# Feed-forward pairs: four of seven products with 512 moving columns, and GpSimd adding sides and scaling gates

## The reference, cut to what matters

```python
def swiglu(x, w_in, w_out):
    gate, up = jnp.split(x @ w_in, 2, axis=-1)
    return (jax.nn.silu(gate) * up) @ w_out
...
h = swiglu(rmsnorm(x, norm_ffn1_pre[l]), w_ffn1_in[l], w_ffn1_out[l])
x = x + FFN_RESIDUAL_SCALE * rmsnorm(h, norm_ffn1_post[l])
```

## Time and profile before

| what | value |
|---|---|
| median of 3 runs | 1515.07 us (1514.86 to 1515.26) |
| the profiled execution's own time | 1514.94 us |
| its span, first to last instruction | 1513.3 us |
| TensorE busy | 1497.9 us, 99% |
| VectorE busy | 1071.1 us, 71% |
| ScalarE busy | 744.2 us, 49% |
| GpSimd busy | 54.2 us, 4% |
| DMA, mean | 101 GB/s |

### The profile page before, as it was taken

The page is one execution under the profiler, slowest core; times in us unless marked ns, Lnnn a source line. Parts: engine busy times, 40 slices in busy tenths (PEclk is TensorE's granted clock), DMA queues, the critical chain, the costliest instruction groups (busy, mean ns, idle before and its releaser), DMA issues.

```text
span 1513.3 us, 23600 instructions
## 1 busy us (share of the span) xinstructions
PE 1497.9 (99%) x9156; PEld 1343.9 (89%) x9156; DVE 1071.1 (71%) x1279; ACT 744.2 (49%) x1102; POOL 54.2 (4%) x101
## 2 busy tenths in 40 slices
PE   8999999999999999999999999999999999999998
PEld 7899998889988889899999888788888888889997
DVE  5888885326856847888886665788888865736873
ACT  6545443226566427544444234567676633344554
POOL 1000000001200002000000000100000000000001
PEclk9999999999999999999999999999999999999999
DMA  6233323232232222233335663222223132322331
GB/s 198 84 112 101 96 81 140 89 105 84 69 103 84 82 101 69 87 109 93 102 111 195 236 208 84 57 65 74 57 82 83 56 111 84 112 85 87 107 112 56
DMA packets 135044, 153.33 MB, mean 101 GB/s; under 512 B 3728, under 2 KB 123660, under 8 KB 134972
## 3 DMA queue, kind: packets, MB, share of 16 engines
q1 hardware_dynamic: 131712, 137.38, 28.9%
q0 software_dynamic: 3024, 14.88, 2.9%
q10 hardware_dynamic: 236, 0.06, 0.0%
HBM read 150.08 MB, written 2.23 MB: 101 GB/s over the span
## 4 chain that ended last, share of the span: by engine, by line
PE 96%; DVE 2%; ACT 1%; issue 0%; DMA 0%; DVEq 0%; ACTq 0%
PE ps L2532 20%; PE ps L2697 20%; PE ps L2534 19%; PE ps L2533 19%; PE ps L2702 10%; PE ps L2897 1%; PE ps L3003 1%; PE ps L3013 1%; PE ps L2983 1%; PE ps L2982 1%; PE ps L3012 1%; PE ps L2615 0%; PE ps L2964 0%; PE ps L2675 0%; DVE wl L1544 0%
## 5 line engine op out<-in xcount | busy, mean ns | idle before, releaser
L2532 PE MATMUL ps<-ah,wh 128*128 128x512 f32 (+1 forms) x1136 | 431.7, 380 | 3.8 <-DVE wl L1945 1.4
L2534 PE MATMUL ps<-ah,wl 128*128 128x512 f32 (+1 forms) x1136 | 425.6, 375 | 0.0
L2533 PE MATMUL ps<-al,wh 128*128 128x512 f32 (+1 forms) x1136 | 425.2, 374 | 0.0
L1544 DVE TENSOR_TENSOR wl<-raw,wh 128x2048 fp32r<-128x2048 f32 x59 | 135.2, 2291 | 191.2 <-ACT wh L831 191.0
L2532 PEld LDWEIGHTS ps<-ah,wh 128*128 128x128 f32 x1136 | 213.9, 188 | 43.3 <-issue 2.3
L2534 PEld LDWEIGHTS ps<-ah,wl 128*128 128x128 f32 x1136 | 213.8, 188 | 38.9
L2533 PEld LDWEIGHTS ps<-al,wh 128*128 128x128 f32 x1136 | 214.1, 188 | 35.5
L831 ACT ACTIVATE wh<-raw 128x2048 fp32r<-128x2048 f32 x60 | 114.7, 1911 | 236.7 <-PE ps L2534 233.0
L2697 PE MATMUL ps<-al,wh 128*128 128x256 f32 x704 | 172.7, 283 | 0.0
L2697 PE MATMUL ps<-ah,wh 128*128 128x256 f32 x704 | 172.7, 283 | 0.0
L2697 PEld LDWEIGHTS ps<-al,wh 128*128 128x128 f32 x704 | 135.2, 192 | 0.1
(11 more groups left out here) (436 smaller groups left out, 2535.6 us busy)
## 6 DMA issues: line engine op xcount, KB each, us to landing
raw<-in_w_ffn_in SPq DMA_DIRECT2D x74, 512.0 KB, 3.6
raw<-in_w_in SPq DMA_DIRECT2D x52, 512.0 KB, 4.4
raw<-in_w_ffn_out SPq DMA_DIRECT2D x22, 1024.0 KB, 5.0
ada_raw<-in_w_ada POOLq DMA_DIRECT2D x8, 1536.0 KB, 7.2
raw<-in_w_mix_in SPq DMA_DIRECT2D x10, 1024.0 KB, 5.4
raw<-in_w_ffn_in SPq DMA_DIRECT2D x7, 1024.0 KB, 5.3
raw<-in_w_in SPq DMA_DIRECT2D x6, 1024.0 KB, 5.6
raw<-in_w_mix_out SPq DMA_DIRECT2D x4, 1024.0 KB, 5.0
```

The costliest lines, as they stand in the source:

```text
L1544: nc.vector.tensor_tensor(wl[n % 2][:], raw[n % 2][:], wh[n % 2][:].bitcast(fp32), ALU.subtract).then_inc(lo_done, 2 if n + 1 in AHEAD else 1)
L2532: nc.tensor.matmul(bank, w[0], m[0], start=start, stop=False, skip_group_check=shared)
L2533: nc.tensor.matmul(bank, w[0], m[1], start=False, stop=False, skip_group_check=shared)
L2534: return nc.tensor.matmul(bank, w[1], m[0], start=False, stop=stop, skip_group_check=shared)
```

## The change

- `ah` and `al` become the two halves of one tile, `both`; `sh` and `sl` of `both_sums`.
- B11, T2, T3 and T4 of the two feed-forward blocks run through a new function, `sided`. Eight matmuls with `wh` move 512 columns each (256 of the high activations and 256 of the low), then eight with `wl` move 256. The result lies in two banks, one for each 128 weight columns (banks 0 and 1, or 6 and 7, by turns of the pair), each with a high side and a low side that must be added.
- ScalarE copies both sides of `up1` and `gate1`, the low side into `acc` and `h7` (`up1_side`, `gate1_side`), and after T4 the low side into `whole2` (`last_side`).
- GpSimd gets four operations a pair: `up1` plus its side, `gate1` plus its side, `gate2` times `rstd`, `gate1` times `rstd`.
- VectorE no longer scales gates. It adds both sides to `gate2`, the second add waiting for the first, and does so ahead of `gate1`, after the fifth product. The second half of `hidden` becomes an add and a multiplication.
- ScalarE takes silu of gate 2 first, and T4 and the next pair's T1 wait for other joins.

```diff
@@ GpSimd @@
+                def added(i, n, step, tile, side):
+                    pool.wait_ge(copied, i * 6 + (3 * n + step))
+                    nc.gpsimd.tensor_tensor(tile[:], tile[:], side, ALU.add).then_inc(side_added, 1)
+                def scaled(i, n, h, tile):
+                    pool.wait_ge(joined, i * 6 + (3 * n + 2 - h))
+                    nc.gpsimd.tensor_tensor(tile[:], tile[:], r_half[h], ALU.mult).then_inc(gate_ready, 1)
+                def pair(i, par):
+                    n = first + par
+                    added(i, n, 1, up1, up1_side)
+                    added(i, n, 3, gate1, gate1_side)
+                    scaled(i, n, 1, gate2)
+                    scaled(i, n, 0, gate1)
...
@@ ScalarE @@
+                def last_side(i, par):
+                    act.wait_ge(hid_ready, i * 2 + (f * NFO + PLAIN[f] + par))
+                    nc.scalar.activation(whole2[:], low_side(par % 2), ACT.Copy).then_inc(side_copied, 1)
...
+                    def sided_product(target, side):
+                        nc.scalar.activation(target[:], high_side(par % 2), ACT.Copy)
+                        nc.scalar.activation(side, low_side(par % 2), ACT.Copy).then_inc(copied, 1)
...
                         used(0)
+                        last_side(i, par - 1)
...
-                    product(up1, BANK1[par % 2])
+                    sided_product(up1, up1_side)
...
-                    product(gate1, BANK1[par % 2])
+                    sided_product(gate1, gate1_side)
                     high(6, i, n)
                     if end:
                         unit(0)
                         unit(1)
-                    gate(0)
                     used(5)
...
                         high(1, i, n + 1)
+                    gate(0)
@@ VectorE @@
+                        dve.wait_ge(side_copied, i * 2 + (n + 1))
+                        nc.vector.tensor_tensor(whole2[:], high_side(par % 2), whole2[:], ALU.add).then_inc(last_joined, 1)
+                        dve.wait_ge(last_joined, i * 2 + (n + 1))
+                        nc.vector.tensor_tensor(at, whole2[:], at, ALU.mult).then_inc(hid_ready, 1)
...
-                    def scaled(tile, h):
-                        dve.wait_ge(joined, i * 6 + (3 * n + h + 1))
-                        nc.vector.tensor_tensor(tile[:], tile[:], r_half[h], ALU.mult).then_inc(gate_ready, 1)
+                    def sided_join(tile):
+                        nc.vector.tensor_tensor(tile[:], high_side(par % 2), tile[:], ALU.add).then_inc(high_joined, 1)
+                        dve.wait_ge(high_joined, i * 2 + (n + 1))
+                        nc.vector.tensor_tensor(tile[:], low_side(par % 2), tile[:], ALU.add).then_inc(joined, 1)
...
-                    used(4)
+                    used(5)
+                    dve.wait_ge(copied, i * 6 + (3 * n + 2))
+                    sided_join(gate2)
                     dve.wait_ge(copied, i * 6 + (3 * n + 3))
+                    dve.wait_ge(side_added, i * 4 + (2 * n + 2))
                     join(gate1, BANK5)
@@ TensorE @@
+            def sided(f, i, n, k, par):
+                moving = both_of(f, PRODUCTS[k])
+                for nb in range(2):
+                    for kk in range(KD // 2):
+                        nc.tensor.matmul(ps[:, SIDE * par + nb, :].rearrange("p (s t) -> p s t", s=2), ring_of(wh, f, k)[:, kk, nb * P:(nb + 1) * P],
+                                         moving[:, :, kk, :], start=k == 0 and kk == 0, stop=False, skip_group_check=True)
+                pe.wait_ge(p_lo, i * 2 * PRODS + (PRODS * n + k + 1))
+                for nb in range(2):
+                    for kk in range(KD // 2):
+                        last = nc.tensor.matmul(ps[:, SIDE * par + nb, 0:T // 2], ring_of(wl, f, k)[:, kk, nb * P:(nb + 1) * P], moving[:, 0, kk, :],
+                                                start=False, stop=kk == KD // 2 - 1, skip_group_check=True)
```

More of the change, by code:

```diff
@@ L115 @@
 BANK1, BANK2, BANK5 = (0, 1), 4, 5
+SIDE = 6
 BRANCH_BANK = (4, 2, 0, 2, 0, 2, 0, 2)
@@ L303, in program @@
             hsl = sb("hsl", [P, 3, KD // 2, T // 2], f32r, where=phase)
+        up1_side, gate1_side = (tile[:].rearrange("p (c t) -> p c t", c=2) for tile in (acc, h7))
         sb2, p2, sz = tt, sq, h7
@@ L543, in weight_of, with high_side, low_side, both_of @@
             return raw_of(f, name)
+        def high_side(par):
+            return ps[:, SIDE * par:SIDE * par + 2, 0:T // 2]
+        def low_side(par):
+            return ps[:, SIDE * par:SIDE * par + 2, T // 2:T]
+        def both_of(f, name):
+            if name == "T3":
+                return both_sums[:, :, 1, :, :]
+            low, high = slice(0, KD // 2), slice(KD // 2, KD)
+            return both[:, :, high if name == "T4" else low, COLS[name != "B11"]]
         def moving_of(f, name):
@@ L760, in ada_load, with sides @@
                 pool.dma_start(ada_raw[:, b, :, :], WAD[:, 4 * b:4 * b + 4, bass.ds(i * ADA, ADA)]).then_inc(ada_in[b], 16)
+            def sides(f):
+                r_half = [rstd[:, COLS[h]].unsqueeze(1).to_broadcast([P, 2, T // 2]) for h in range(2)]
+                first = SEVEN_AT[f]
+                def added(i, n, step, tile, side):
[10 more added lines that the diff above has]
+                    scaled(i, n, 0, gate1)
+                pool.wait_ge(gt_done, PLAIN_AT[f] + PLAIN[f])
+                pair(0, 0)
+                pair(0, 1)
+                with pool.Fori(1, SEVEN[f] // 2) as i:
+                    pair(i, 0)
+                    pair(i, 1)
+                if SEVEN[f] % 2:
+                    pair(SEVEN[f] // 2, 0)
+            sides(0)
             pool.wait_ge(rlo_done, 2)
@@ L781, in _ @@
             add_residual(3)
+            sides(1)
             pool.wait_ge(p_used, PRODS * (SEVEN[0] + SEVEN[1]))
@@ L2692, in products @@
                     pe.wait_ge(p_hi, i * 2 * PRODS + (PRODS * n + k + 1))
+                    if f < 2 and name in ("B11", "T2", "T3", "T4"):
+                        sided(f, i, n, k, par)
+                        continue
                     high, low = moving_of(f, name)
@@ L2799, in free @@
                     elif c == BANK5:
-                        pe.wait_ge(joined, 3 * (SEVEN_AT[f] + SEVEN[f]) - 2)
+                        pe.wait_ge(joined, 3 * (SEVEN_AT[f] + SEVEN[f]) - 1)
                     elif c == BANK2:
                         pe.wait_ge(joined, 3 * (SEVEN_AT[f] + SEVEN[f]))
-                    elif c == BANK1[1 - SEVEN[f] % 2]:
+                    elif c == earlier:
+                        pe.wait_ge(hid_ready, (f + 1) * NFO - 1)
+                    elif c == later:
                         pe.wait_ge(hid_ready, (f + 1) * NFO)
-                unit(0, first=True, blocks=[6, 7, 2, 3, BANK1[SEVEN[f] % 2], BANK5, BANK2, BANK1[1 - SEVEN[f] % 2]], before=free)
+                earlier, later = SIDE * (SEVEN[f] % 2), SIDE * (1 - SEVEN[f] % 2)
+                unit(0, first=True, blocks=[2, 3, earlier, earlier + 1, BANK5, BANK2, later, later + 1], before=free)
                 with pe.Fori(0, 4) as i:
```

32 lines of the change are left out of this document (16 added, 16 removed).

## The result

The changed kernel takes 1529.99 us (median of 4 runs, 1528.00 to 1530.88) against 1514.99 before (4 runs, 1514.86 to 1515.26): 1.0097 times, 95% interval 1.0079 to 1.0114. The profiled execution is the one of 1530.88, with a span of 1529.2. The forecast was 1521 in a range of 1511 to 1532: the direction is right, the loss twice and a half what was forecast (15.9 us in the profiled execution in place of 6.4).

A forecast was written before the change was run, and what follows sets the result against it. TensorE, busy 99%, bounds the kernel before; after, VectorE does, with 16.96 + 3.4 = 20.4 us a pair against TensorE's 19.73. Each block ends 3.2 us later, +6.4 on 1514.94: 1521 us, range 1511 to 1532.

The forecast's parts named there:

- TensorE's saving: Four products of a pair use 512-column matmuls: 0.107 us less a product, pairs of 19.73 us for 20.16, 7.7 us saved.
- The turns of GpSimd and VectorE: In the pairs, GpSimd's calls hold up VectorE's two-tile operations: 3.4 us a pair, mean 0.85 a call.
- The rule's full 1.29: VectorE loses the add's whole 1.29 us at each call, about 1553 us; within the 0.03 chance of above 1536.
- VectorE's own work: VectorE's operations in a pair, without GpSimd's calls: 16.7 us plus 0.24 for two followers, 16.96 us.
- forecast start of the out stage: End of each block: VectorE's summed work lets the out stage start at 184.6 us instead of 181.4, 3.2 later.
- TensorE's waits: TensorE idles some 0.6 us a pair at T2 from the third pair, and about 3 us before each out stage.
- dearer calls: GpSimd's calls cost VectorE more than forecast, the kernel taking 1528 to 1536 us; chance 0.20.
- No price: Rival: GpSimd's calls cost VectorE nothing, TensorE sets the pairs, 1508.6 us; chance 0.12.
- Near break-even: Rival: calls cost VectorE 0.70 to 0.80 us, around the break-even of 0.76, giving 1512 to 1518 us; chance 0.13.
- every call at 1.03: Rival: each of 36 calls a block costs VectorE 1.03 us, 1534 us; dearer calls of 1528 to 1536 had chance 0.20.

The follow-up runs named there:

- e1_small: The changed kernel with each of GpSimd's four calls a pair cut from 256 to 4 columns of each half; 1510.17 us, ratio to before 0.9968.
- e3_vector: The changed kernel with all four GpSimd operations given to VectorE and silu of gate 1 first again; 1509.63 us, ratio to before 0.9964.
- e4_fill: The changed kernel with 14 unused matmuls of 512 columns ahead of the wait at each out stage; 1526.53 us, ratio to before 1.0076.
- e2_memset: The changed kernel with each GpSimd call cut to 4 columns and a memset over the other 252 of each half; 1510.2 us.
- e6_scale: The kernel before with only the scaling of both gates moved from VectorE to GpSimd; 1515.73 us, ratio 1.0004.
- e5_more: The changed kernel with a fifth GpSimd call a pair, a two-tile 128x512 add whose result nobody uses; 1549.08 us, ratio 1.0222.

## Why the prediction was right in kind and short in size

*TensorE's saving.* Forecast 0.107 us a product. A sided product's eight wide matmuls begin 1.84 us ahead of the next ones, so 0.230 each in place of 0.2267: 0.08 us a product, pairs of 19.8 in place of 19.73. Right to 2 us in the whole kernel, and seen only where VectorE doesn't hold it (e1_small, e3_vector).

*The turns of GpSimd and VectorE.* Forecast from two rows of adds elsewhere in the trace: 1.03 us in the open, 0.65 beside a PSUM read, 3.4 a pair. Measured 1.09 and 1.10 in the open, 0.53 and 0.72 beside one, 3.44 a pair. This term stands, call by call. The rule's full 1.29 did not come.
The Trainium skill (SBUF — State Buffer, SBUF: two separate sides) speaks of the whole instruction as the loser's wait. In the rows above turns are whole, and the loser pays 1.10 us beside a call of 1.29, so the lock is borne out, and the full 1.29 that the prediction took from it is, by these rows, a little high.

*VectorE's own work.* This term was too small: 16.96 us a pair forecast, 17.18 measured. The steps were counted at 1.135 and 0.605, with 0.12 for each of two followers. But the sum into `tt` waits, by a semaphore of the kernel (`p_lo`), for the low part that reads `tt`: 1.24 us from start to start (142.86 to 144.10) in place of 1.135. And the last multiplication follows its add by 0.82 (146.99 to 147.81), not 0.72. The first could have been read in before's own trace:

```profile
140.04 1.22 DVE L1776 TENSOR_TENSOR wl<-tt,wh 128x1024 fp32r<-128x1024 f32 x1 [1.14 <-ACT wh L1002]
141.29 1.23 DVE L1788 TENSOR_TENSOR tt<-raw 128x1024 f32<-128x1024 f32 x1
```

Nine pairs make 9 x 0.22 = 2.0 us of it a block, and the calls 9 x 0.04 = 0.4 more. The forecast start of the out stage, 184.6, becomes 187.0; it was 187.2 and 186.9. A saturated engine passes all of a small error on: the blocks end 11.2 us later in place of 6.4, 4.8 more.

*TensorE's waits.* T2 waits 0.6 us for the copy of `up1` from the third pair on, and the out stage waits 3.15: as forecast.

*What the sum did not have at all.* The wait of 3 us was forecast and taken at its own length. What it brings, the granted clock at its lower level for 6.8 and 3.4 us, costs 4.4 us more (3.0 and 1.4), and e4_fill, which removes it, is 4.4 us faster. Forecast 6.4, own work and calls 4.8, clock 4.4, and 0.3 at the waits' ends: 15.9. The range held the result only because it reached to dearer calls, a case that did not happen. That it held is luck in part: 1530 came of two things that the sum had too small or not at all.

*The rivals.* No price, 1508.6: e1_small and e3_vector show that this is where the kernel would be without the turns (1510.2 and 1509.6). Near break-even and every call at 1.03: neither, the mean was 0.86. The break-even price a call, forecast 0.76, is in truth about 0.71, since VectorE's own work is 2.0 us a block longer (2.0 / 36 = 0.055).

## What to carry to other kernels

Offloading to GpSimd is no offload when VectorE is full of operations that read two SBUF tiles and GpSimd reads SBUF too: a 128x512 operation costs VectorE 0.6 us at home and 0.5 to 1.1 us away. Count what the engine loses, not what it hands over. What cost no time here was GpSimd work that reads next to nothing (e2_memset) or that falls into VectorE's idle time (e6_scale). And when a forecast has TensorE wait 3 us at one place, look at what a matmul costs behind the wait, not only at the wait.

## What the runs showed of the hardware

- In waits of 3.15 and 3.17 us the granted clock fell to half 2.5 and 2.6 us after the last matmul's end, and stayed there for 6.8 and 3.4 us. Waits of up to 0.6 us (12 of them) left it at 1.00 in the same kernel. e5_more waits 3.35 us there and falls as well (0.50 in the window 256 to 262). The two stretches differ by a factor of two after equal waits; why was not settled.
- A GpSimd memset (128x504, 0.52 us) costs a two-tile VectorE operation nothing. A one-tile copy takes 0.60 us alone, 1.60 where such an operation goes first, and costs VectorE 0.2 to 0.4 us where the copy goes first. A two-tile add or multiplication (128x512, 1.29 us alone) costs it 1.09 to 1.14 when it goes first and nothing covers it.
- On GpSimd, multiplying by a row repeated over two halves costs VectorE as much as an add of two whole tiles (+1.10).
